# 225 products behind the last real one, with weights that lie apart, are one number, or are few

## The chip, the cores and the metric

The kernel runs on one core of a Trainium2 chip. The metric is the device time of one execution in microseconds (us); lower is better. The time of before is 3466.73 us, the median of two runs (3463.19 and 3470.27).

## What is computed

Two transformer-like networks, one behind the other, over one sequence of 512 tokens with 1024 features, in f32. The first has two layers of gated feed-forward, sparse attention beside a gating MLP, and feed-forward again. The second has two layers as well; its last piece, with which the kernel ends, is

```python
m_lat = sq_relu_mlp(modulate(rms_norm(x, g_mlp_pre[i]), sh2, sc2), w_mlp_in[i], w_mlp_out[i])
x = x + gt2 * rms_norm(m_lat, g_mlp_post[i])
```

where `sq_relu_mlp` is `square(relu(h @ w_in)) @ w_out` with 4096 hidden features. What is added by the change is no part of this: its results stay in two banks that nobody reads.

## The kernel before, in words

Activations lie feature-major: a tile `[128, 8, 512]` holds 8 blocks of 128 features by 512 tokens. Every matrix product of weights is made from three passes. ScalarE rounds a raw weight tile to `WH` (line 557, a type that TensorE streams at full rate), VectorE makes the rest `WL = raw - WH` (line 568), and the activations are split in the same way, into `nH` and `nL`. A product is then WH x nH + WH x nL + WL x nH, three matmuls that add up in one PSUM bank (lines 662 to 664, and likewise 1039 to 1041, 2483 to 2485, 2778 to 2780). In `pe.q.matmul(out, weights, moving)` the second argument is the stationary one, which is loaded into the array by a weight load (engine PEld in the profile), and the third is streamed past it, one column after the other. "512 columns" is the width of the moving argument. All weights of these products are `[128, 128]` pieces whose 128 numbers lie next to each other in each partition.

There are four buffers for `WH` and four for `WL` (`NW = 4`), each `[128, 2048]`, used in turn. `M.ones` is a `[128, 128]` f32 tile of ones; with it sums over partitions are made, and also products that only keep TensorE at work (`warm_up`, line 682, and line 1440).

Each engine has its program, a Python function that issues its instructions in the order in which they stand: `pe_program`, `act_program`, `dve_program`, `pool_program`, `sp_program`. Semaphores tie them together; `then_inc` counts one up, `wait_ge` waits for a value. PSUM has eight banks. Six go round in `now.order`: `take` hands out the next one and returns with it the event that empties it, on which the caller waits before it writes. Banks 6 and 7 hold the two `stat` tiles of the halves of the sequence.

TensorE's program ends in `rest_pe`, whose last call is `mlp2_turn_pe`, the last feed-forward. It ends in `turn_pe` (lines 2512 to 2533): eight blocks of 128 output features for the first half of the tokens, eight for the second, each of 24 matmuls of 256 columns (lines 2483 to 2485), and then the norm of the second half: `half_sum_pe` (line 877, sums by weights times a column of ones) and `half_spread_pe` (line 882, one product with the tile of ones, which spreads the inverse root over all partitions). VectorE adds each block into `ma` (line 2730 of `into_sums`, which empties the bank and counts up `v_h`), and at the very end multiplies by the spread norm (line 2696) and adds to `h` (line 2701), from where SyncE stores it.

The names of the change: `lat.nH` and `lat.nL` are the split activations, `[128, 8, 512]` each; `M.WH[0]` and `M.WL[0]` the first of the four weight buffers, which no later step of the kernel writes at that place; `mm` TensorE's semaphore.

Of the kernel before, what the change touches and what calls it, by code (L numbers as in the profile page):

```python
# [234 lines left out]
def drain(steps):  # L235
    for _ in steps:
        pass


def weave(main, side, pace):  # L240

    n, live = 0, [True, True]
    while live[0] or live[1]:
        for which, steps, c in ((0, main, 1), (1, side, pace(n) if live[0] else 1)):
            for _ in range(c):
                if live[which]:
                    try:
                        next(steps)
                    except StopIteration:
                        live[which] = False  # L250
        n += 1
# [158 lines left out]
def build(nc, A, out):  # L410
# [3 lines left out]
    with ctx:  # L414
        M = memory(nc, ctx)
        lat, con, key = M.lat, M.con, M.key
        sems = {}

        def sem(name):
            sems[name] = Sem(ctx.enter_context(nc.semaphore(name)))  # L420
            return sems[name]
# [15 lines left out]
        mm = sem("mm")  # L437
# [29 lines left out]
        def take(*group):  # L467

            b = now.order.pop(0)
            now.order.append(b)  # L470
            bank_of[group] = b
            before = now.holder.get(b)
            now.holder[b] = group
            if before is None:
                return banks[b], (mm.handle, 0)
            if COUNTING[0]:
                return banks[b], (mm.handle, 1)
            return banks[b], emptied_by[before].to(*before)
# [51 lines left out]
        offs, at = [], 0  # L530
# [1020 lines left out]
        def network_pe(pe, l, j):  # L1551
            g = f"ffn{l}{j}"
            if l == j == 0:
                start_pe(pe)
            else:
                enter_pe(pe, l, 2 * j)
            yield from ffn_pe(pe, g, lat, g, NF, True, "ffn_w_in", "ffn_w_out", M.hH, M.hL, l + j > 0, l * j == 0,
                              begun=l == j == 0)
# [672 lines left out]
        def mixer_pe(pe, l):  # L2231
            g = f"mix{l}"
            enter_pe(pe, l, 1)
            attention1_pe(pe, g, l)
            gmlp_pe(pe, g)
            for m in range(4):
                for which in range(2):
                    if m or which:
                        merge_pe(pe, g, which, m)
# [272 lines left out]
        def turn_pe(pe, post, g, group, clear):  # L2512

            A, B = lat.half

            def first_sum():
                pe.wait_ge(*clear[0])
                half_sum_pe(pe, post + "A", A)

            for o in range(8):  # L2520
                group(pe, 0, o)
            for o in range(8):
                group(pe, 1, o, first_sum if o == 0 else None)
                if o == 0:
                    half_spread_pe(pe, post + "A", A)
                if o == 5 and g is not None:
                    half_sum_pe(pe, g + "A", A)
                if o == 6 and g is not None:
                    half_spread_pe(pe, g + "A", A)
            pe.wait_ge(*clear[1])  # L2530
            if g is None:
                half_sum_pe(pe, post + "B", B)
                half_spread_pe(pe, post + "B", B)
# [204 lines left out]
        def mlp2_turn_pe(pe, g, after, lead):  # L2738
            yield from ffn_pe(pe, g, lat, g, NF2, False, "w_mlp_in_2", "w_mlp_out_2", M.hH2, M.hL2, lead > 0, True, lead)
            extra = narrow()  # L2740
            turn_pe(pe, g + "post", after, second_end_pe(g), [emptied(x) for x in extra])
# [138 lines left out]
        def context_pe(pe):  # L2880
            yield from pooled_pe(pe)
            yield from norm_pe(pe, "ctxmlp", con)
# [47 lines left out]
        def latents_pe(pe):  # L2930
            for s in range(LATENTS_STEPS):
                if s == 4:
                    b, free = take(FIN, "sum")
                    pe.wait_ge(*free)
                    pe.wait_ge(*v_ssum.to(FIN, 7))
                    pe.wait_ge(*v_ssum.to(POOL2, 7))
                    for j in range(4):
                        c = slice(j * 128, j * 128 + 128)
                        pe.q.matmul(b[:, j:j + 1], lat.scr[2][:, c], M.ones[:, 0:1], start=True, stop=True)
                        pe.q.matmul(b[:, 4 + j:5 + j], M.fin[2][:, c], M.ones[:, 0:1], start=True, stop=False)  # L2940
                        t = pe.q.matmul(b[:, 4 + j:5 + j], lat.scr[2][:, c], M.epsc[:, 0:1], start=False, stop=True)
                    t.then_inc(*mm.up(FIN, "sum"))
                if s == 5:
                    spread_pe(pe, POOL2, M.fin[3])
                    spread_pe(pe, FIN, lat.scr[3])
                    put_back(FIN, "rstd")
                if s == 8:
                    put_back(POOL2, "rstd")
                if s in POOLED_STEPS:
                    pool_out_pe(pe, POOL2, POOLED_STEPS.index(s), M.gH, M.gL, S)  # L2950
                if s == 19:
                    sum_pe(pe, POST2, M.fin[2])
                if s == 20:
                    spread_pe(pe, POST2, lat.scr[3])
                if s == 27:
                    put_back(POST2, "rstd")
                    sum_pe(pe, MLP2, M.fin[2])
                if s == 28:
                    spread_pe(pe, MLP2, lat.scr[3])
                if s == 32:  # L2960
                    put_back(MLP2, "rstd")
                yield
# [325 lines left out]
        def tail_pe(pe):  # L3288
            g, p = "ctxkey", key
            yield from norm_pe(pe, "ctxmlppost", p)  # L3290
            yield from norm_pe(pe, g, p)
            xs, ready = normed_x(p, g)
            slot_pair(pe, "w_qkv_2", C, xs, ready, [("kc0", "raw"), ("kc1", "raw")])
            yield
            slot_pair(pe, "w_qkv_2", C, xs, ready, [(g, "v", i) for i in range(2)])
            yield
            for name in ("kc0", "kc1"):
                head_pe(pe, p, name)
            yield
            values_pe(pe, g, p)  # L3300
            yield
            yield
            for name in ("kc0", "kc1"):
                head_spread_pe(pe, p, name)
            yield
# [43 lines left out]
        def latents_on_pe(pe):  # L3349
            yield from mlp2_turn_pe(pe, "latmlp0", "latatt", 0)  # L3350
# [303 lines left out]
        def rest_pe(pe, output):  # L3654
            turn_pe(pe, "wopost", "latmlp1", output, [a_ev.to("y2", hh) for hh in (6, 7)])
            after_turn_pe(pe, "w_mlp_in_2", "wopost", "latmlp1", FIRST_HIDDEN)
            drain(mlp2_turn_pe(pe, "latmlp1", None, 3))
# [35 lines left out]
        def beside_context(n):  # L3693
            return 1

        def pe_program(pe):
            pe.wait_ge(*v_one.to("ones"))
            for l in range(2):
                drain(network_pe(pe, l, 0))
                pe.wait_ge(*ld_id.to())  # L3700
                mixer_pe(pe, l)
                if l == 0:
                    drain(network_pe(pe, l, 1))
            weave(network_pe(pe, 1, 1), context_pe(pe), beside_network)
            weave(context_on_pe(pe), latents_pe(pe), beside_context)
            weave(latents_on_pe(pe), tail_pe(pe), beside_context)
            rest_pe(pe, attention2_pe(pe))

        def act_program(act):
            act.wait_ge(*v_one.to("eps"))  # L3710
            for l in range(2):
                drain(network_act(act, l, 0))
                act.wait_ge(*ld_vec.to())
                mixer_act(act, l)
                if l == 0:
                    drain(network_act(act, l, 1))
            weave(network_act(act, 1, 1), context_act(act), beside_network)
            weave(context_on_act(act), latents_act(act), beside_context)
            weave(latents_on_act(act), tail_act(act), beside_context)
            attention2_act(act)  # L3720
            rest_act(act)
# [105 lines left out]
        for program in (pe_program, act_program, dve_program, pool_program, sp_program):  # L3827
            program(Lane(Tally()))
# [3 lines left out]
        block = ctx.enter_context(nc.Block())  # L3832
# [114 lines left out]
```

## Time and profile before

| | us |
|---|---|
| median of the runs shown | 3466.73 |
| the profiled execution | 3466.52 |
| its span, first to last instruction | 3464.7 |
| TensorE busy | 3413.6 (99%) |
| weight loads busy | 2874.5 (83%) |
| VectorE busy | 2165.7 (63%) |
| ScalarE busy | 1318.4 (38%) |

The rows below come from that execution. A row of a timeline gives the start in us from the span's start, the duration, engine, line, operation and tiles. TensorE's matmuls are pipelined: a record lasts from its start to the end of its results, and the next one begins before that. So what a matmul costs in a stream is the distance between starts, not the duration of a record. A product of two plain f32 tiles (the ones) stands in the trace as two records. PEclk and the clock column are the clock that TensorE was granted, as a share of 2.4 GHz.

### The profile page before, as it was taken

The numbers are of one execution on the slowest core, as the hardware profiler recorded it, in microseconds if no ns is written. First come the engines' busy times: TensorE is split into PE (matmuls) and PEld (weight loads), VectorE is DVE, ScalarE is ACT, GpSimd is POOL, SyncE is SP. The second block draws the span as 40 slices with busy tenths as digits, with TensorE's granted clock in tenths as the row PEclk, the third lists the DMA queues.
The fourth block names the chain that finished last, engine by engine and source line by source line (L and its number), as shares of the span: only waits on it lengthen the run. The fifth ranks groups of instructions, "written<-read, shape, count | busy, mean of one in ns | idle before, by whom it ended". The sixth has DMA issues, their size and how long they took to land.

```text
span 3464.7 us, 46915 instructions
## 1 busy us (share of the span) xinstructions
PE 3413.6 (99%) x18494; PEld 2874.5 (83%) x18494; DVE 2165.7 (63%) x3570; ACT 1318.4 (38%) x1951; POOL 298.0 (9%) x376
## 2 busy tenths in 40 slices
PE   9999999999999999999999999999999999999998
PEld 7888967898888988896789888899988898588888
DVE  7555565656555655666577777888776556655444
ACT  4222463333222422245333523355533236643222
POOL 0000232001000100023100000012100001210000
PEclk9999999999999999999999999999999999999999
DMA  7444302434444344320243444344444311013221
GB/s 279 188 158 163 107 24 101 163 129 168 158 162 151 134 169 158 148 106 12 101 164 140 149 150 170 146 147 182 172 174 165 117 66 68 25 50 112 96 98 48
DMA packets 85561, 452.01 MB, mean 130 GB/s; under 512 B 10304, under 2 KB 12544, under 8 KB 48608
## 3 DMA queue, kind: packets, MB, share of 16 engines
q1 hardware_dynamic: 83168, 439.10, 34.2%
q0 software_dynamic: 2176, 9.92, 0.8%
q8 instruction: 148, 2.42, 0.3%
q14 instruction: 69, 0.57, 0.0%
HBM read 446.88 MB, written 2.10 MB: 130 GB/s over the span
## 4 chain that ended last, share of the span: by engine, by line
PE 84%; DVE 7%; ACT 3%; issue 2%; DMA 2%; POOL 0%; SPq 0%; DVEq 0%; ACTq 0%; POOLq 0%
PE ps L662 21%; PE ps L663 21%; PE ps L664 21%; DVE WL L568 2%; DMA araw<-in_ast 2%; PE ps L2778 1%; PE ps L2780 1%; PE ps L2779 1%; PE ps L3477 1%; PE ps L1039 1%; PE ps L1040 1%; PE ps L1041 1%; ACT P L1859 1%; PE ps L1776 1%; PE ps L1299 1%
## 5 line engine op out<-in xcount | busy, mean ns | idle before, releaser
L662 PE MATMUL ps<-nH,WH 128*128 128x512 f32 x2256 | 880.3, 390 | 0.4 <-ACT rot L3207 0.4
L664 PE MATMUL ps<-nH,WL 128*128 128x512 f32 x2256 | 877.8, 389 | 0.0
L663 PE MATMUL ps<-nL,WH 128*128 128x512 f32 x2256 | 877.8, 389 | 0.0
L568 DVE TENSOR_TENSOR WL<-raw,WH 128x2048 fp32r<-128x2048 f32 (+2 forms) x297 | 651.6, 2199 | 361.5 <-ACT WH L557 360.0
L557 ACT ACTIVATE WH<-raw 128x2048 fp32r<-128x2048 f32 (+2 forms) x299 | 543.2, 1822 | 561.1 <-PE ps L664 479.9
L662 PEld LDWEIGHTS ps<-nH,WH 128*128 128x128 f32 x2256 | 423.5, 188 | 90.6 <-issue 3.3
L664 PEld LDWEIGHTS ps<-nH,WL 128*128 128x128 f32 x2256 | 423.4, 188 | 88.3
L663 PEld LDWEIGHTS ps<-nL,WH 128*128 128x128 f32 x2256 | 423.5, 188 | 87.2 <-issue 0.2
L628 DVE SCALAR_TENSOR_TENSOR araw<-araw,cB 128x1024 f32<-128x1024 f32 x224 | 275.6, 1230 | 205.6 <-DMA araw<-in_ast 205.2
L662 PE MATMUL ps<-hH,WH 128*128 128x512 f32 x944 | 368.8, 391 | 2.5 <-DVE ma L2454 1.4
L664 PE MATMUL ps<-hH,WL 128*128 128x512 f32 x944 | 367.4, 389 | 0.0
L663 PE MATMUL ps<-hL,WH 128*128 128x512 f32 x944 | 367.2, 389 | 0.0
L1146 ACT ACTIVATE scr<-ps 128x512 f32<-128x512 f32 x152 | 89.5, 595 | 414.4 <-PE ps L664 387.2
L1012 POOL TENSOR_SCALAR scr<-scr,der,mods 128x256 f32<-128x256 f32 x112 | 86.2, 771 | 1805.8 <-DVE scr L925 1804.8
L1153 ACT ACTIVATE hH<-scr 128x512 fp32r<-128x512 f32 x152 | 95.8, 633 | 357.5 <-DVE scr L1199 355.5
L662 PEld LDWEIGHTS ps<-hH,WH 128*128 128x128 f32 x944 | 177.2, 188 | 40.3 <-DVE ma L2454 1.9
L664 PEld LDWEIGHTS ps<-hH,WL 128*128 128x128 f32 x944 | 177.2, 188 | 36.9
L663 PEld LDWEIGHTS ps<-hL,WH 128*128 128x128 f32 x944 | 177.2, 188 | 36.6
L1199 DVE TENSOR_TENSOR scr<-scr,ps 128x512 f32<-128x512 f32 x88 | 59.5, 687 | 108.4 <-PE ps L664 107.0
L1266 DVE SCALAR_TENSOR_TENSOR h<-ps,der,h 128x512 f32<-128x512 f32 x144 | 99.7, 746 | 27.2 <-PE ps L664 25.9
L1202 DVE TENSOR_TENSOR scr<-scr 128x512 f32<-128x512 f32 x64 | 43.1, 690 | 101.3 <-ACT scr L1146 100.9
L1208 DVE TENSOR_TENSOR hL<-scr,hH 128x512 fp32r<-128x512 f32 x152 | 100.8, 687 | 4.3
(452 smaller groups left out, 5940.0 us busy)
## 6 DMA issues: line engine op xcount, KB each, us to landing
raw<-in_wst SPq DMA_DIRECT2D x273, 1024.0 KB, 4.8
araw<-in_ast SPq DMA_DIRECT2D x225, 512.0 KB, 5.7
raw<-in_wst SPq DMA_DIRECT2D x18, 512.0 KB, 3.3
araw<-in_wst SPq DMA_DIRECT2D x9, 1024.0 KB, 4.8
row<-in_ast SPq DMA_DIRECT2D x15, 512.0 KB, 10.5
cw<-in_cw POOLq DMA_DIRECT2D x4, 1024.0 KB, 5.9
h<-in_xT SPq DMA_DIRECT2D x4, 512.0 KB, 5.6
raw<-in_wst SPq DMA_DIRECT2D x8, 256.0 KB, 2.6
```

Of the source, the lines that this page charges most:

```text
L557: act.q.activation(M.WH[k % NW][:, 0:n], M.raw[raw_use[k]][:, 0:n], ACT.Copy).then_inc(*a_whi.up(k))
L568: dve.q.tensor_tensor(M.WL[k % NW][:, 0:n], M.raw[raw_use[k]][:, 0:n], M.WH[k % NW][:, 0:n].bitcast(F32), ALU.subtract).then_inc(*v_wlo.up(k))
L628: dve.q.scalar_tensor_tensor(out=w[:, :], in0=w[:, :], scalar=1.0, in1=M.cB[q][:, :], op0=ALU.mult, op1=ALU.mult, accum_out=total).then_in ...
L662: pe.q.matmul(to, hi[:, i, cc], xh, start=i == 0, stop=False)
L663: pe.q.matmul(to, hi[:, i, cc], xl, start=False, stop=False)
L664: t = pe.q.matmul(to, lo[:, i, cc], xh, start=False, stop=i == nk - 1)
L1012: pool.q.tensor_scalar(p.scr[2 + i % 2][:, p.cols], p.scr[i % 2][:, p.cols], G[:, i:i + 1], shift[:, i:i + 1], ALU.mult, ALU.add).then_inc ...
L1146: act.q.activation(p.scr[n % 2][:, 0:N], bank(g, "a", ci, f)[:, 0:N], ACT.Silu if gated else ACT.Relu).then_inc(*empties(a_fn, g, "a", ci, f))
L1153: act.q.activation(hH[:, ci % 2, f, :], p.scr[(2 if gated else 0) + f % 2][:, 0:N], ACT.Copy if gated else ACT.Square).then_inc(*a_hhi.up( ...
L1199: dve.q.tensor_tensor(p.scr[2 + u][:, 0:N], p.scr[u][:, 0:N], bank(g, "b", ci, f)[:, 0:N], ALU.mult).then_inc(*empties(v_pr, g, "b", ci, f))
L1208: dve.q.tensor_tensor(hL[:, ci % 2, f, :], p.scr[2 + f % 2][:, 0:N], hH[:, ci % 2, f, :].bitcast(F32), ALU.subtract).then_inc(*v_hlo.up(g, ...
L1266: dve.q.scalar_tensor_tensor(out=M.h[:, o, :], in0=bank(g, "o", ci, o)[:, :], scalar=gate[:, o:o + 1], in1=M.h[:, o, :], op0=ALU.mult, op1 ...
```

## The change

A function `end_pe` is called as TensorE's last step, behind `rest_pe`. It takes two banks and issues, in this order:

- 20 times two products of ones by ones (`between`), into the second bank;
- 25 groups of nine products each into the first bank, each group followed by two products of ones. The nine are three blocks i = 0, 1, 2, and for each the three passes of a real product (WH x nH, WH x nL, WL x nH). The moving operand starts at number 512 i + 16 x `line` of the tile;
- one last product of ones, which counts up a semaphore for which nobody waits.

The groups differ in their weights and their columns:

| groups | columns | weights |
|---|---|---|
| 4 | 512 | 128, every second number of 256 |
| 4 | 512 | 128, every fourth number of 512 |
| 2 | 512 | 128 times one number |
| 2 | 512 | 64 next to each other |
| 1 | 512 | 32 next to each other |
| 8 | 256 | 128, every second number |
| 4 | 256 | 128, every fourth number |

```diff
+        def end_pe(pe):
+
+            nh, nl = (x[:, :, :].rearrange("p a b -> p (a b)") for x in (lat.nH, lat.nL))
+            two = [take("end", x) for x in range(2)]
+            for b, free in two:
+                pe.wait_ge(*free)
+            to, aside = two[0][0], two[1][0]
+
+            def between():
+                for _ in range(2):
+                    pe.q.matmul(aside[:, 0:128], M.ones[:, :], M.ones[:, :], start=True, stop=True)
+
+            def apart(w, i, step):
+                return w[:, 512 * i:512 * i + 128 * step].rearrange("p (a b) -> p a b", b=step)[:, :, 0]
+
+            def block(w, i, rows):
+                return w[:, 128 * i:128 * i + rows]
+
+            def one(w, i, _):
+                return w[:, 512 * i:512 * i + 1].broadcast_to([128, 128])
+
+            def nine(N, line, weights, how, rows=128):
+                for i in range(9):
+                    w, x = ((0, 0), (0, 1), (1, 0))[i % 3]
+                    at = 512 * (i // 3) + 16 * line
+                    pe.q.matmul(to[0:rows, 0:N], weights(M.WL[0] if w else M.WH[0], i // 3, how),
+                                (nl if x else nh)[:, at:at + N], start=i == 0, stop=i == 8)
+                between()
+
+            for _ in range(20):
+                between()
+            for line in range(4):
+                nine(512, line, apart, 2)
+            for line in range(4):
+                nine(512, line, apart, 4)
+            for line in (0, 1):
+                nine(512, line, one, 0)
+            for line in (0, 3):
+                nine(512, line, block, 64, 64)
+            nine(512, 0, block, 32, 32)
+            for line in range(8):
+                nine(256, line, apart, 2)
+            for line in (0, 1, 2, 3):
+                nine(256, line, apart, 4)
+            t = pe.q.matmul(aside[:, 0:128], M.ones[:, :], M.ones[:, :], start=True, stop=True)
+            t.then_inc(*mm.up("end", 1))
...
             rest_pe(pe, attention2_pe(pe))
+            end_pe(pe)
```

Line 3706 is the product of ones in `between`, line 3721 the product in `nine`, line 3740 the last one. On TensorE the seam between the old program and the new instructions looks so, with the semaphores that are waited for (`v_dg` is VectorE's count of the inverse roots; `WH_7` and `WL_11` are the first weight buffers):

```order
 L877 MATMUL ps<-ones,scr_26 128x1
 L882 MATMUL ps<-scr_27,ones 128x256 [waits v_dg]
+L3706 MATMUL ps<-ones 128x128 [waits v_h]
+L3706 MATMUL ps<-ones 128x128 x39
+L3721 MATMUL ps<-nH,WH_7 128x512
+L3721 MATMUL ps<-nL,WH_7 128x512
+L3721 MATMUL ps<-nH,WL_11 128x512
```

The first added instruction carries the only wait of the addition. Behind the last product of the last group, of 256 columns, TensorE's program now ends in this way, where `L414` is the end of the block for all engines:

```order
+L3721 MATMUL ps<-nH,WH_7 128x256
+L3721 MATMUL ps<-nL,WH_7 128x256
+L3721 MATMUL ps<-nH,WL_11 128x256
+L3706 MATMUL ps<-ones 128x128 x2
+L3740 MATMUL ps<-ones 128x128
 L414 UNCONDITIONAL_BRANCH
```

Nothing moved: before, the branch stood directly behind line 882. The orders of the other engines are the same but for line numbers, which are 48 higher behind the new function.

## Rows read from the trace of the kernel before

**Rows 1.** The page's head and its table of busy time by engine

```profile
span 3464.7 us, 46915 instructions
...
PE 3413.6 (99%) x18494; PEld 2874.5 (83%) x18494; DVE 2165.7 (63%) x3570; ACT 1318.4 (38%) x1951; POOL 298.0 (9%) x376
```

**Rows 2.** Groups by line and shape: out<-in, count | busy us, mean ns | idle before

```profile
L662 PE MATMUL ps<-nH,WH 128*128 128x512 f32 x2256 | 880.3, 390 | 0.4 <-ACT rot L3207 0.4
...
L1039 PE MATMUL ps<-nH,WH 128*128 128x256 f32 x320 | 92.1, 288 | 0.3
...
L1641 PE MATMUL ps<-R,cw 128*128 128x62 f32 x128 | 14.7, 273 | 0.0
...
L663 PEld LDWEIGHTS ps<-nL,WH 128*128 128x128 f32 x2256 | 423.5, 188 | 87.2 <-issue 0.2
...
L1039 PEld LDWEIGHTS ps<-nH,WH 128*128 128x128 f32 x320 | 61.4, 192 | 0.9 <-issue 0.8
...
L2101 PEld LDWEIGHTS ps<-wT,vn 128*64 128x64 f32 x128 | 6.9, 137 | 0.7 <-issue 0.7
```

**Rows 3.** Timeline of TensorE, first and last of 46 products of 512 columns

```profile
599.79 0.39 PE L662 MATMUL ps<-nH,WH 128*128 128x512 f32 x1
...
609.99 0.39 PE L662 MATMUL ps<-yaH,WH 128*128 128x512 f32 x1
```

**Rows 4.** Timeline of the tail, from the last products of 256 columns to the end

```profile
3450.81 0.28 PE L2484 MATMUL ps<-hL,WH 128*128 128x256 f32 x1
...
3452.01 0.28 PE L2485 MATMUL ps<-hH,WL 128*128 128x256 f32 x1
3452.33 0.42 DVE L2730 TENSOR_TENSOR ma<-ma,ps 128x256 f32<-128x256 f32 x1 [2.12 <-PE ps L2485]
...
3453.80 0.58 PE L877 MATMUL ps<-ones,scr 128*128 128x1 f32 x4 [1.51 <-DVE scr L908]
...
3455.45 1.22 PE L882 MATMUL ps<-scr,ones 128*128 128x256 f32 x2 [1.07 <-DVE scr L916]
3456.70 0.69 DVE L2696 TENSOR_TENSOR ma<-ma,ps 128x512 f32<-128x512 f32 x1 [1.31 <-PE ps L882]
...
3458.15 4.34 SPq L3820 DMA_DIRECT2D out<-h  x4
...
3461.40 0.69 DVE L2701 TENSOR_TENSOR h<-h,ma 128x512 f32<-128x512 f32 x1
```

**Rows 5.** Windows: stretch, its length, busy us (records) by engine, PEclk, DMA share, GB/s

```profile
3440.00:3446.00 6.00, 6.00 (x52) 6.00 (x51) 2.73 (x7) 1.86 (x4) 0.00 (x0) 1.00 0.21 68
3456.00:3465.00 9.00, 0.67 (x2) 0.00 (x0) 5.25 (x8) 0.00 (x0) 0.00 (x0) 0.50 0.34 117
...
600.00:609.90 9.90, 9.90 (x45) 8.20 (x44) 8.80 (x17) 0.59 (x2) 0.00 (x0) 1.00 0.00 0
...
18.80:21.30 2.50, 2.50 (x14) 2.50 (x13) 0.50 1.03 408
21.60:23.20 1.60, 1.60 (x15) 1.42 (x13) 1.00 1.06 266
```

**Rows 6.** Timeline of DVE: blocks 2 and 3 of the second half leave their banks

```profile
3437.93 0.42 DVE L2730 TENSOR_TENSOR ma<-ma,ps 128x256 f32<-128x256 f32 x1 [0.76 <-PE ps L2485]
...
3440.81 0.42 DVE L2730 TENSOR_TENSOR ma<-ma,ps 128x256 f32<-128x256 f32 x1 [0.41 <-PE ps L2485]
```

**Rows 7.** Timeline of TensorE near the start: products of ones

```profile
18.53 4.69 PE L682 MATMUL ps<-ones 128*128 128x128 f32 x28
...
26.23 3.29 PE L1440 MATMUL ps<-ones 128*128 128x128 f32 x28
```

**Rows 8.** Timeline of TensorE, first and last of nine products of the context

```profile
2349.17 0.28 PE L2779 MATMUL ps<-hLc,WH 128*128 128x256 f32 x1
...
2350.11 0.28 PE L2778 MATMUL ps<-hHc,WH 128*128 128x256 f32 x1
```

## Prediction

> **What bounds the kernel now.** I read the page's table of engines first. TensorE is busy 99% of a span of 3464.7 us with 18494 matmul records [rows 1], so anything that is put on TensorE and isn't beside a wait of TensorE lengthens the kernel. The change adds only TensorE work, and only behind the last instruction that TensorE has. So two things are to be read: what one product of each shape costs in a dense stream, and how much of the tail, in which TensorE is idle already, the addition can use.
>
> The mean durations by shape (390 ns for 512 columns, 288 ns for 256) [rows 2] are no prices, since records overlap. The price is the distance from start to start. In the timeline 45 products of 512 columns start between 599.79 and 609.99 us: 10.20 / 45 = 0.2267 us each [rows 3]. At 256 columns, 10 products start between 3450.81 and 3452.01 us: 0.1200 each [rows 4]. The difference, 106.7 ns for 256 columns, is 0.417 ns a column, one column per clock at the higher level of 2.4 GHz, at which these stretches are granted (1.00 in [rows 5]). What is left is a price per product that doesn't depend on its columns: 226.7 - 512 x 0.417 = 13.3 ns. On this number the forecast turns, because the new products change only their weights.
>
> The tail: TensorE's last real product starts at 3452.01 us. DVE, ACT and TensorE then pass the last norm to each other, TensorE's last two records (one product of `M.ones`) run from 3455.45 to 3456.67, and DVE and the output DMAs fill the rest up to 3464.7 [rows 4]. There the granted clock is 0.50, the lower level of 1.2 GHz [rows 5], after TensorE had been mostly idle from 3452.3 to 3455.45. So 3464.7 - 3456.5 = 8.2 us of the addition cost nothing, whatever it is.
>
> **The change part by part.** Nothing is removed or moved; the other engines' instructions stand as before. Four things are added.
>
> *The wait.* `end_pe` takes two banks and waits for `v_h`. The two that come next held blocks 2 and 3 of the second half, which DVE read (L2730) at 3437.93 and 3440.81 us [rows 6], over 14 us before TensorE gets there. The wait costs nothing, and nothing is queued behind it but the addition. No engine waits for the semaphore at its end. I let the addition start at 3456.5.
>
> *The 40 lead-in products of ones.* A product of two plain f32 tiles is two records in the trace: the 14 products of L1440 are 28 records, and they take 0.111 us each ((3.29 - 0.28) / 27) at the higher clock [rows 7]. At the lower level 14 records touch a stretch of 2.50 us where at the higher 15 touch 1.60 [rows 5], so about 0.2 each. How long the lower level lasts I take from the start of this kernel, where it is still 0.50 up to 21.30 and 1.00 from 21.60 the ones there having begun at 18.53 [rows 5, 7]: some 3 us. So of 80 records 14 at 0.213 and 66 at 0.1115: 3.0 + 7.4 = 10.4 us, up to 3466.9.
>
> *The separators.* 25 x 2 products are 100 records x 0.1115 = 11.15 us; the last product 0.22, and 0.28 until its record ends.
>
> *The 225 products.* If weights apart cost what contiguous ones do: 13 groups x 9 x 0.2267 = 26.52, and 12 x 9 x 0.1200 = 12.96. TensorE then ends at 3466.9 + 26.5 + 13.0 + 11.2 + 0.5 = 3518.1. The profiled execution took 3466.52 us over a span of 3464.7, so 1.8 lie around it, and its time is 0.2 below the median: 3519.9.
>
> No row of before shows weights that aren't contiguous, so their price is bounded. From below: the 13.3 ns go altogether, 225 x 13.3 = 3.0 us less (a gain). From above: a weight load is a record of 188 to 192 ns that today lies wholly beside the product before it [rows 2]; if none of it did, the 180 products with weights apart would cost 180 x 0.19 = 34 us more. Between them I ask what the 13.3 ns are. The timeline of the context's products has the same weight tiles, columns and engine but other moving tiles, and there 8 products take 2350.11 - 2349.17 = 0.94, 0.1175 each [rows 8]: the constant is 10.8 ns there. A price that depends on which tile streams past is not a fixed cost of an instruction; it looks like the reading of weights getting in the way of the reading of the moving tile. Then it should grow with the stretch of memory the weights lie in. I take that: x2 for every second number, x4 for every fourth, none for one number, a half and a quarter for 64 and 32. So +13.3 ns x (36 + 72) = 1.4 us, +40 ns x (36 + 36) = 2.9, -13.3 x 18 = -0.2, -6.7 x 18 - 10 x 9 = -0.2; together +3.9, and 3523.7 us. It is also near the middle of what is likely and far nearer to the free end than to 34.
>
> Weight loads of 64 columns take 137 ns against 192 for 128, 0.86 ns a column, and 128 products of only 62 columns still take 14.7 us, 0.115 each, much like the ones with their 0.111: there the loads of 128 columns set the pace [rows 2]. The Trainium skill, "TensorE: Matmul & The Clock Gate", section "LDWEIGHTS (loading the stationary operand)", has the same: the load's time is its columns over 1.2 GHz, and nothing else. By it alone weights apart are free, as in the first rival. Against this change stands "Advanced Engine Details and Errata", section "SBUF Cachelines": lines of 16 bytes, and a reader needs "at least two hits on a cacheline to absorb SRAM access latency". f32 at every second number is two hits a line, at every fourth one; no run here shows it yet.
>
> **The rivals.**
>
> 1. *Weights apart cost what contiguous ones do.* For it: loads have their own record beside the products and are off TensorE's path everywhere. Against it: 0.1175 against 0.1200 with equal shapes. 3519.9 us, still slower but within 2%.
>
> 2. *Loads at every fourth number take twice as long, and become the bound of the short products.* A load comes each 0.111 us at best; twice that, 0.223, hides behind 512 columns (0.2267) and not behind 256 (0.1200). Price: 36 x 0.103 = 3.7 us on top of rival 1: 3523.6. Only where the time sits tells it from my forecast. The rule on cachelines above would give this.
>
> 3. *The other side: loads of weights apart aren't hidden.* If a strided load holds up the product behind it by a load's whole pace, 180 x 0.1115 = 20.1 us more than rival 1: 3540.0, +2.1%, slower by over 2%. It decides from (3536.1 - 3519.9) / 180 = 0.09 us a product. For it speaks only that no strided load is in the trace; against it that loads begin with the product before them and have 0.2267 us of room at 512 columns, in 72 of the 180.
>
> 4. *The clock stays at its lower level.* Columns then cost 0.417 ns more: 117 x 512 and 108 x 256 columns make 25.0 + 11.5, and 100 records 0.1 more each, 10: about 3570 us, +3%. Against it: the same string of ones brings the clock back within some 3 us at the kernel's start [rows 5], and the products that follow have no wait among them.
>
> That the addition does nothing to the time can't be: it would have to fit into 8.2 us.
>
> **How the numbers follow.** Price by the stretch of memory (forecast, 3523.7): 0.38. Rival 1: 0.25. Rival 2: 0.20. Rival 3: 0.11. Rival 4: 0.03. What I haven't thought of: 0.03, of it 0.01 faster. The range goes from the free end (3519.9 less 3.0 for the constant and 1.4 if the clock never falls: 3515) to just under rival 3: 3539. It leaves out rivals 3 and 4 and the 34 us of the upper bound, some 0.17. By 2%, which is about what a measurement of this kernel can tell from no change, faster is below 3397.4 and slower above 3536.1: faster 0.01, same 0.85, slower 0.14.
>
> **What would show it.** Distances from start to start in the new groups. By my forecast at 512 columns: every second 0.240, every fourth 0.267, one number 0.213, 64 weights 0.220, 32 weights 0.217; at 256 columns 0.133 and 0.160. By rival 1: 0.227 and 0.120 throughout. By rival 2: 0.227 at 512 columns, and 0.223 for every fourth at 256, where every second stays at 0.120. By rival 3: 0.34 and 0.23. The lead-in should end about 11.5 us after TensorE's last record of before began, and the granted clock be 1.00 from the first group on. I am wrong in the main step if one number costs as much as 128 contiguous ones, or if every fourth costs the same as every second; wrong in the frame if the first added product waits, or if separators cost more than 0.1115 a record behind products of another kind.

## The result, and the profile after

The changed kernel takes 3523.72 us, the median of two runs (3522.63 and 3524.80), against 3466.73 before: a ratio of 1.0164, 95% interval 1.0118 to 1.0211. Run again beside the experiments, four times, it took 3523.69 (1.0165, 1.0148 to 1.0182). It is slower by 57 us. The second interval lies wholly under a ratio of 1.02; the first, of two runs, reaches just past it. The predicted time was 3523.7. That it fits so well is partly luck, as the terms below show: the step on which the sum turned was wrong.

The profiled execution of after is the one of 3522.63 us. The head of its page answers to [rows 1]; TensorE has 407 records more, 225 products and twice 91 products of ones.

```profile
span 3520.8 us, 47730 instructions
...
PE 3481.1 (99%) x18901; PEld 2937.4 (83%) x18901; DVE 2166.2 (62%) x3570; ACT 1319.1 (37%) x1951; POOL 298.9 (8%) x376
```

Windows of the new tail answer to [rows 5]; the columns are those of there.

```profile
3453.10:3456.40 3.30, 3.30 (x14) 3.12 (x15) 2.07 (x4) 0.00 (x0) 0.00 (x0) 0.50 0.00 0
3456.50:3464.00 7.50, 7.50 (x70) 7.50 (x69) 3.08 (x5) 0.00 (x0) 0.00 (x0) 1.00 0.43 142
3464.00:3520.00 56.00, 56.00 (x327) 50.98 (x326) 0.00 (x0) 0.00 (x0) 0.00 (x0) 1.00 0.00 1
```

The clock is low for some 3 us, comes back early among the ones and stays. VectorE and the output are done under the lead-in. From 3464 on TensorE alone works, with no gap.

The chain of work that ended last is the best view for the groups, because it gives each group's time from end to end: start, us, what. The 13 groups of 512 columns, then the 12 of 256:

```profile
3453.01 1.22 PE ps L882 x2
3454.23 10.03 PE ps L3706 x80
3464.25 2.11 PE ps L3721 x9
3466.37 0.44 PE ps L3706 x4
...
3474.43 2.23 PE ps L3721 x9
...
3485.19 2.07 PE ps L3721 x9
...
3490.25 2.06 PE ps L3721 x9
...
3497.85 1.08 PE ps L3721 x9
...
3510.08 2.11 PE ps L3721 x9
...
3520.30 0.22 PE ps L3740 x2
```

They are the first groups of their kinds: every second number (3464.25), every fourth (3474.43), one number (3485.19), 64 weights (3490.25), and at 256 columns every second (3497.85) and every fourth (3510.08). Nine products of 256 columns take 1.08, as contiguous ones would (9 x 0.120), with every second number, and 2.11 with every fourth: 0.234 a product, twice the price, and as much as 512 columns cost. One number at 512 columns takes 2.07, not 1.92.

The groups by weight load say why. The first row is of the stretch of 512 columns at every second number, the second of every fourth at 512, the third of every second at 256, the fourth of every fourth at 256.

```profile
L3721 PEld LDWEIGHTS ps<-nL,WH 128*128 128x128 f32 x12 | 2.3, 196 | 0.3
...
L3721 PEld LDWEIGHTS ps<-nL,WH 128*128 128x128 f32 x12 | 3.8, 317 | 0.0
...
L3721 PEld LDWEIGHTS ps<-nL,WH 128*128 128x128 f32 x24 | 4.7, 196 | 0.0
...
L3721 PEld LDWEIGHTS ps<-nL,WH 128*128 128x128 f32 x12 | 4.0, 331 | 0.0
```

Contiguous weights were 188 to 192 [rows 2]. Every second number adds some 5 ns, every fourth 120 to 140.

### The profile page after: what moved, and what is told of

It is laid out like the page before. It is cut to its first block, busy times and chain, and to the rows that moved or that the text cites. A ratio compares the mean times of both kernels' runs of the same rounds, so it can differ in the third digit from the quotient of the medians.

```text
span 3520.8 us, 47730 instructions
## 1 busy us (share of the span) xinstructions
PE 3481.1 (99%) x18901; PEld 2937.4 (83%) x18901; DVE 2166.2 (62%) x3570; ACT 1319.1 (37%) x1951; POOL 298.9 (8%) x376
## 4 chain that ended last, share of the span: by engine, by line
PE 86%; DVE 6%; ACT 3%; issue 2%; DMA 1%; POOL 0%; SPq 0%; DVEq 0%; ACTq 0%; POOLq 0%
PE ps L662 21%; PE ps L664 21%; PE ps L663 21%; PE ps L2778 1%; PE ps L2780 1%; PE ps L2779 1%; DVE WL L568 1%; PE ps L3721 1%; PE ps L3477 1%; DMA araw<-in_ast 1%; PE ps L1039 1%; PE ps L1040 1%; PE ps L1041 1%; PE ps L1776 1%; ACT P L1859 1%
```

## The experiments

Theory L, formed from these rows: a load of weights at every fourth number has half the pace, and a product costs the larger of its load and its columns; the 13.3 ns of [rows 3, 4] have nothing to do with weights. Theory S is the one that I predicted with: the 13.3 ns grow with the stretch of memory that the weights lie in. All kernels change `end_pe` alone; the kernel's real work is untouched, and the results of the added products are read by nobody. The kernels from "Long runs" on were timed once each, and only distances inside their traces are read.

**The changed kernel again**

No edit.

> The changed kernel unaltered, beside the two that follow, so that they have one chip and one time to be compared with. Every theory: 3523.7 us within 2; the start-to-start distances as in its first trace, by group about 0.233 (512 columns, every second number), 0.238 (every fourth), 0.231 (one number, 64, 32 weights), 0.120 (256 columns, every second), 0.234 (256 columns, every fourth).

Measured: 3523.69 us (3521.48 to 3526.46), each group within 0.03 us of the first trace.

**Weights next to each other**

```diff
-            for line in range(4):
-                nine(512, line, apart, 2)
-            for line in range(4):
-                nine(512, line, apart, 4)
+            for line in range(8):
+                nine(512, line % 4, block, 128)
...
-                nine(256, line, apart, 2)
+                nine(256, line, block, 128)
...
-                nine(256, line, apart, 4)
+                nine(256, line, block, 128)
```

> All weights that lie apart are replaced by 128 that lie next to each other; the groups, columns, moving tiles and separators stay. Theory L (a load at every fourth number has half the pace, every second number is free, and the 13.3 ns have nothing to do with the weights): the eight groups of 512 columns take 2.49 to 2.55 us each with their separators, the twelve of 256 columns 1.53 each, so only the eight groups at every fourth number give something back, 4 x 0.15 + 4 x 1.02 = 4.7 us, and the kernel takes 4 to 6 us less than the changed one. Theory S (my prediction: the 13.3 ns grow with the stretch of memory the weights lie in): 3.9 us less than the changed one, of which 1.4 from the groups at every second number, whose short groups fall from 1.65 to 1.53. Rival N (strided weights cost nothing and the long groups are slow for another reason): the same time within 1 us.

Measured: 3519.86 us (3517.05 to 3520.15), 3.8 less than the changed kernel on the same chip. The chain, with a group of 512 columns in place of every second number, one in place of every fourth, and the same at 256 columns:

```profile
3463.78 2.08 PE ps L3721 x9
...
3473.91 2.07 PE ps L3721 x9
...
3496.67 1.08 PE ps L3721 x9
...
3508.73 1.07 PE ps L3721 x9
```

What falls is what L says: the groups at every fourth number, by 1.05 us at 256 columns and 0.16 at 512 on average, together 4.8. Every second number gives back only 0.01 to 0.02 a group: at 256 columns the eight groups took 1.08 or 1.09 and take 1.04 to 1.08 now. By the medians alone L and S, 4.7 and 3.9, can't be told apart; by the rows S falls, for it wanted 1.20 (9 x 0.133) where 1.08 stood. N falls too.

**No lead-in**

```diff
-            for _ in range(20):
-                between()
```

> The 40 products of ones ahead of the groups are left out; the groups follow the last real product at once. If the clock comes back with any dense work: some 10.0 us of lead-in go, and the first 2 to 5 us of products run at the lower level at twice their time, which gives back 1.2 to 2.5: 7.5 to 9 us less than the changed kernel. If it takes the string of ones to bring the clock back (the groups stay at the lower level): 117 x 0.213 + 108 x 0.107 + 100 x 0.1 = 46 us more instead of 10 less, 36 us more than the changed kernel.

Measured: 3516.12 us (3510.19 to 3519.75), 7.6 less. The windows of the first group and of the next four have the clock at 0.50 and at 1.00:

```profile
3455.00:3457.70 2.70, 2.70 (x8) 2.11 (x7) 2.63 (x5) 0.00 (x0) 0.00 (x0) 0.50 0.26 89
3458.50:3468.90 10.40, 10.40 (x55) 9.36 (x53) 1.49 (x3) 0.00 (x0) 0.00 (x0) 1.00 0.21 71
```

In the chain the first group alone is slow:

```profile
3454.60 3.64 PE ps L3721 x9
```

The second takes 2.10 again. The lead-in's term was right, and rival 4 falls: products bring the clock back as ones do. A side result counts later. The timeline has the group's inner products, of which the second and the eighth are

```profile
3454.82 0.63 PE L3721 MATMUL ps<-nL,WH 128*128 128x512 f32 x1
...
3457.38 0.63 PE L3721 MATMUL ps<-nL,WH 128*128 128x512 f32 x1
```

At the lower level they start 2.56 / 6 = 0.427 us apart, which is 512 columns at 1.2 GHz and nothing on top. The 13.3 ns are gone there.

**Long runs**

```diff
+            run(45, 512, block, 128)
+            run(45, 512, block, 32, 32)
+            run(45, 512, one, 0)
+            run(45, 512, apart, 2)
+            run(45, 512, block, 128, one_moving=True)
+            run(45, 512, block, 128, bank=(to, aside))
+            run(45, 512, block, 128, tile=M.hH2[:, :, :, :].rearrange("p a b c -> p (a b c)"))
+            run(45, 384, block, 128)
+            run(45, 256, block, 128)
+            run(45, 256, block, 32, 32)
+            run(45, 256, one, 0)
```

These stand in place of the groups.

> Instead of the 25 groups eleven runs of 45 products each, with two products of ones behind each. 512 columns: 128 contiguous weights; 32 weights; one number; every second number; contiguous with one moving tile throughout; contiguous with two banks in turn; contiguous with the hidden activations as moving tile. Then 384 and 256 columns contiguous; 256 with 32 weights; 256 with one number. Theory L, 13.3 ns is not the weights': contiguous, 32, one number and every second number all settle at 0.2267 at 512 columns, 0.120 at 256, and 384 columns take 0.1733. Theory S: one number 0.2133 to 0.216, 32 weights 0.217, every second number 0.240. If the 13.3 ns come from adding up in one bank, the run with two banks settles near 0.216; if from reading two moving tiles in turn, the run with one tile does; if from where the moving tile lies, the run with the hidden activations differs from the first. If the 0.231 to 0.233 of the groups of nine is a matter of being short, each run begins so and settles within some ten products.

Measured, from the chain: 512 columns with 128 contiguous weights, with one number, with every second number; then 256 columns with contiguous weights and with one number:

```profile
3465.54 10.25 PE ps L3734 x45
...
3487.11 10.43 PE ps L3734 x45
...
3497.98 10.50 PE ps L3734 x45
...
3549.22 5.40 PE ps L3734 x45
...
3560.63 5.12 PE ps L3734 x45
```

Contiguous weights begin between 0.22 and 0.24 and settle at 0.2267 after some ten products; so a group of nine never gets to the price that [rows 3] show. One number, and 32 weights in the same way (10.43), don't settle and stay at 0.232, dearer than 128; every second number stays at 0.233. At 256 columns it is the other way round: one number takes 5.12 / 45 = 0.1138, 32 weights too, against 0.1200 for 128. Neither L, by which the weights don't count, nor S, by which fewer are always cheaper, has these 5 to 6 ns, and no later run explains them. 384 columns take 7.81 / 45 = 0.1736, which is still 384 x 0.417 + 13.3. The bank, one moving tile or two, and the tile itself make no difference (10.23 or 10.24).

**Spacing of the weights**

```diff
+            for step in (1, 2, 3, 4, 5, 6, 8, 15):
+                nine(128, 0, step)
+            for at in (1, 2, 3):
+                nine(128, at, 3)
+            for step in (1, 2, 3, 4, 5, 6, 8, 15):
+                nine(256, 0, step)
+            for at in (1, 2, 3):
+                nine(256, at, 3)
+            for n in (64, 32):
+                nine(256, 0, 4, False, n)
+            for N in (128, 256):
+                for step in (1, 2, 4, 6, 8, 16):
+                    nine(N, step > 1, step, True)
```

In place of the groups; `True` is bf16, with ones as moving tile.

> Groups of nine as in the change, one for each spacing of the weights. First 128 columns, f32 at every 1st, 2nd, 3rd, 4th, 5th, 6th, 8th, 15th number, then every 3rd from numbers 1, 2, 3; the same at 256 columns; 64 and 32 weights at every 4th number at 256 columns; then bf16 weights (one bf16 is half an f32) at every 1st, 2nd, 4th, 6th, 8th, 16th at 128 and 256 columns. Theory P (a pair rule: two weights within 16 bytes load at full pace, one weight per 16 bytes at half): at 128 columns 0.111 for 1st and 2nd, something between for 3rd, 0.233 for 4th and everything beyond, with no further growth; bf16 slow from the 8th on, not at the 4th. Theory G (pace grows with the stretch): 3rd about 0.17, 4th 0.23, 8th 0.46, 15th 0.9. Theory C (a count of numbers, not bytes): bf16 is slow from the 4th on like f32. 64 and 32 weights at every 4th number at 256 columns: loads need half and a quarter of the time and hide, about 0.120, by P and C.

Measured: at 128 columns the first four groups, every 1st, 2nd, 3rd, 4th number; then at 256 columns the 4th and 15th; then bf16 at 128 columns, 6th and 8th:

```profile
3467.06 0.96 PE ps L3718 x9
...
3468.51 1.01 PE ps L3718 x9
...
3470.02 1.51 PE ps L3718 x9
...
3472.03 2.10 PE ps L3718 x9
...
3501.21 2.11 PE ps L3718 x9
...
3511.39 2.10 PE ps L3718 x9
...
3526.09 0.50 PE ps L3718 x9
...
3527.09 0.55 PE ps L3718 x9
```

The distances inside the first four are 0.111, 0.118, 0.173 and 0.234. 128 weights at every 2nd, 3rd, 4th number touch 64, 96, 128 stretches of 16 bytes, and 118 / 64 = 1.84, 173 / 96 = 1.80, 234 / 128 = 1.83 ns. So a load of this type costs the larger of its columns (0.111) and some 1.82 ns for each 16 bytes that it touches. Beyond every 4th nothing grows with the spacing (2.06 to 2.18 from the 5th to the 15th): G falls. bf16 is slow only from the 8th on, which is 16 bytes again: C falls. But it is slow at another price: 0.55 / 9 = 0.061 us for 128 stretches is 0.48 ns each, where 1.82 would make 0.233. Why a bf16 load is so much quicker is open; the 1.82 ns are shown for weights of the kernel's type alone. 64 and 32 weights at every 4th number hide, 1.06 and 1.07. P is right, for this type in a sharper form. The Trainium skill has the 16 bytes and the two hits ("Advanced Engine Details and Errata", section "SBUF Cachelines"), and this trace agrees, with 1.82 ns as the price for this type. The statement of the Trainium skill that a load's time is its columns ("TensorE: Matmul & The Clock Gate", section "LDWEIGHTS (loading the stationary operand)") holds only for weights next to each other.

**Columns**

```diff
+            for step in (1, 4):
+                for N in (128, 192, 256, 320, 384, 448, 480, 512):
+                    for line in (0, 1):
+                        nine(N, line, apart, step)
```

> Contiguous weights, then every fourth number, at 128, 192, 256, 320, 384, 448, 480 and 512 columns, two groups of nine each. Theory L (a load at every fourth number is slow by itself, and a product costs the larger of its columns and its load): every fourth 0.233 at all widths up to 480, 0.238 at 512; contiguous 0.111 at 128 and 192 (load), 0.117 to 0.120 at 256, then 0.147, 0.173, 0.200, 0.213, 0.230. Rival K (strided loads are slow only because they meet the stream of the moving tile): every fourth grows with the columns, below 0.17 at 128 columns and near 0.233 only at 256 and beyond.

Measured: every fourth number at 128 and 384 columns, first group each:

```profile
3497.20 2.05 PE ps L3721 x9
...
3517.67 2.16 PE ps L3721 x9
```

Behind the first product, which starts late, the distance is on average 0.233 to 0.236 up to 384 columns and 0.234 to 0.239 from 448 on. The load is slow by itself; K falls. Contiguous weights fit at 320 and 384 columns (0.147, 0.174), but at 448 one of two groups took 0.206 and at 480 both took 0.218, more than columns plus 13.3.

**Steps of 16 columns?**

```diff
+            for spread in (0, 1):
+                for N in (248, 252, 256, 260, 264, 272, 288, 496):
+                    run(27, N, 0, spread)
+            for spread in (0, 1):
+                for start in (1, 4, 8, 16, 32):
+                    run(27, 256, start, spread)
```

`spread` 0 is one number as weights, 1 is 128 contiguous ones.

> What the 13.3 ns behind the columns are. Runs of 27 products at 248, 252, 256, 260, 264, 272, 288 and 496 columns, first with one number as weights and then with 128 contiguous ones; then at 256 columns with the moving tile beginning 1, 4, 8, 16 and 32 numbers further on, again with both kinds of weights. Theory Q (a product takes whole steps of 16 columns, 6.7 ns, and one or two steps more than its columns): one number gives 0.1133 for 248, 252 and 256 columns and 0.120 for 260 to 272, in steps. Theory F (a fixed price on top of the columns): 0.417 ns for each column, 248 and 256 columns 3.3 ns apart. If the reading of weights gets in the way of the moving tile only where both begin alike, the runs with contiguous weights vary with the start and those with one number don't.

Measured with one number, at 248, 260, 288 and 496 columns:

```profile
3468.66 3.06 PE ps L3714 x27
...
3479.25 3.22 PE ps L3714 x27
...
3490.42 3.56 PE ps L3714 x27
...
3494.43 6.11 PE ps L3714 x27
```

That is 0.1133, 0.1193, 0.1319 and 0.2263 a product: not steps, and not a fixed price, for what is left over the columns is 10 ns at 248 and 20 at 496. But divided by the stretches of 16 bytes of the *moving* tile, 62, 65, 72 and 124, it is 1.83 ns each time. Of the other four widths three lie between 1.82 and 1.84, and 256 columns at 1.79. With 256 columns (64 stretches) runs lie between 0.1141 and 0.1226 by start and weights; at each of the six starts the contiguous weights are dearer than one number, by 1 to 5 ns, while at 496 columns they are cheaper (0.2233). So the weights keep a small say, which no run explains. Q and F are both wrong, and 1.83 is the price that a stretch of weights of this type has, too.

**The moving tile**

```diff
+            run(27, every(1, 512))
+            run(27, one_number(512))
+            run(27, each(4))
+            run(27, again(4))
+            run(27, every(1, 256))
+            run(27, one_number(256))
+            for step in (2, 3, 4, 8):
+                run(27, every(step, 256))
+            for step in (2, 4, 8):
+                run(27, every(step, 256, 1), kind=BF16)
+            for step in (1, 2, 4):
+                run(9, every(step, 256), kind=F32)
```

> The weights are 128 contiguous ones throughout; what changes is how the moving tile lies in memory, in runs of 27 products (the last three of 9). 512 columns: contiguous; one number for all columns; 128 numbers, each four times in a row; 128 numbers gone through four times. 256 columns: contiguous; one number; every 2nd, 3rd, 4th, 8th number. bf16 at 256 columns: every 2nd, 4th, 8th. Plain f32 (two records a product) at 256 columns: every 1st, 2nd, 4th. Theory R (TensorE reads a stretch of 16 bytes, four f32, in about 1.82 ns whatever it takes from it; a product costs the larger of its columns at 0.417 ns with 2.5 on top, the stretches of its moving tile and those of its weights): 512 contiguous 0.227 to 0.233; one number 0.216; each four times 0.216; gone through four times 0.227 to 0.233; 256 contiguous 0.117 to 0.120; one number 0.111; every 2nd 0.233, 3rd 0.350, 4th and 8th 0.466; bf16 2nd 0.117, 4th 0.233, 8th 0.466; plain f32 0.215, 0.233, 0.466. Rival F (the 13.3 ns are a fixed price of a product of this type): 0.227 and 0.120 for one number as for contiguous, and strides of the moving tile of any price. Rival H (only the weights' reader has a pace by stretches): the moving tile's spacing changes nothing.

Measured, the four runs of 512 columns; 256 columns contiguous, from one number, and at every 2nd and 4th number; bf16 at every 2nd, 4th and 8th:

```profile
3463.33 6.14 PE ps L3722 x27
...
3469.91 5.85 PE ps L3722 x27
...
3476.21 5.83 PE ps L3722 x27
...
3482.48 6.14 PE ps L3722 x27
...
3489.07 3.24 PE ps L3722 x27
...
3492.75 3.02 PE ps L3722 x27
...
3496.21 6.12 PE ps L3722 x27
...
3509.34 6.29 PE ps L3722 x27
...
3522.41 3.06 PE ps L3722 x27
...
3525.91 6.16 PE ps L3722 x27
...
3532.52 12.21 PE ps L3722 x27
```

512 columns from 128 numbers, each four times in a row, take 0.2159, and from one number 0.2167: columns plus 2.6 to 3.4 ns. The same 128 numbers gone through four times, 128 stretches again, take 0.227, as contiguous ones do (6.14 both). 256 columns from one number take 0.112, contiguous 0.120. So the 13.3 ns are, but for those 3 ns, the reading of the moving tile and no fixed price: F falls. bf16 at every 2nd, 4th, 8th number takes 0.113, 0.228, 0.452, which is 64, 128 and 256 stretches at 1.77 to 1.78 ns each; plain f32 0.216, 0.227, 0.451 a record. H falls. R fails at one place: the products' own type at every 3rd, 4th and 8th number takes 0.227, 0.233 and 0.218 where R wanted 0.350 and 0.466. Why that type reads spaced columns faster than the others is open, and so for this type the price by stretches is shown only for moving tiles that are contiguous, repeated, or at every 2nd number.

## Why the prediction was right, and where it was wrong

The terms, forecast against the profiled execution of after. The times are from one chain start to that of the next kind.

| term | forecast us | measured us |
|---|---|---|
| start of TensorE's last product of before | 3455.45 | 3453.01 |
| from there to the first group | 11.45 | 11.24 |
| 512 columns, every second, 4 groups | 10.4 | 10.18 |
| 512 columns, every fourth, 4 groups | 11.4 | 10.76 |
| one number, 64, 32 weights, 5 groups | 12.0 | 12.66 |
| 256 columns, every second, 8 groups | 13.2 | 12.23 |
| 256 columns, every fourth, 4 groups | 7.5 | 10.22 |

**What bounds the kernel** held: nothing on another engine came into play, and the time is TensorE's. **The wait** held: the added instructions follow the last real one with no gap. **The lead-in** held within 0.3 us, and its removal gave 7.6 where 7.5 to 9 was expected. **The separators** held: 0.44 for four records, 0.111 each.

**The step that failed** is this: "it looks like the reading of weights getting in the way of the reading of the moving tile. Then it should grow with the stretch of memory the weights lie in." The forecast put 13.3 ns a product on the weights and scaled them. By the last two experiments the 13.3 ns at 512 columns are the moving tile's own reading, 128 stretches of 16 bytes at 1.77 ns instead of 512 columns at 0.417. With one number as weights they don't go: its groups took 2.07 and 2.09 us and contiguous ones 2.07 to 2.11, the sign that I had named for being wrong in the main step. Two widths, 512 and 256, gave me a slope and an offset, and 384 columns, at 0.1736, lie on the same line; it took 248 and 496 columns, 10 and 20 ns over their columns, and moving tiles that lie otherwise to show that the offset is no fixed price. The observation under the step, that the context's tile has another price [rows 8], was sound, and pointed to the moving side.

The weights do cost by the stretch of memory, but in their own reading, beside the products: 1.82 ns for each 16 bytes, 118 ns at every second number and 234 at every fourth, which shows only where it is more than the product costs. So every second number is hidden under 0.120 but for some 2 ns, and every fourth is not. That is rival 2, forecast at 0.223 a product and measured at 0.234, with its price where it put it: the short groups at every fourth number cost 1.05 us more each than contiguous ones, 4.2 in all, where my theory had 0.36 each. I gave it 0.20.

The sum came out because the errors cancel. The four short groups at every fourth number are 2.7 under; the eight at every second are 0.9 over, the first two kinds 0.9 over, one number and few weights 0.7 under. These sum to 1.6 too little, and this execution's real work ended 2.4 us earlier than the one I started from, with 0.2 from the lead-in: 3523.7 + 1.6 - 2.6 = 3522.7, against 3522.63. The 0.2 us by which the profiled execution lies below the median stand in the forecast's words, but not in its 3519.9. A size not in any forecast is that groups of nine are too short to settle, 2.52 us where nine times 0.2267 and the separators make 2.49.

Rival 1 gave 3519.9 us, which is what the kernel with contiguous weights takes (3519.86); for the changed kernel it is 3.8 us short. Rival 3, loads that aren't hidden, is wrong: at 512 columns every fourth number cost 0.16 us a group, not 1.0. Rival 4 is wrong by the run without lead-in. The range held, and the chances by 2% were placed rightly: the price that would have crossed it, 0.09 us on each of 180 products, came on 36 of them only.

## What to carry to other kernels

Price a matmul of this kernel's type in a dense stream by the largest of three: its columns, the 16-byte stretches of its moving operand, and those of its weights (here 1.77 to 1.84 ns each). Behind the first product of a group that comes out within 10 ns in these runs, with two exceptions: a moving operand of this type at every 3rd number or further apart costs less, and bf16 weights have a lower price. Weights at every second f32 are free to within 2 ns in the short groups and cost 6 ns in a long run of 512 columns; at every fourth they cost a product of 256 columns twice its time. bf16 weights became dearer only at every 8th number, by 6 ns at 128 columns. A line through a few widths doesn't make what is left over a fixed price: let the operand lie otherwise in memory and see whether it goes. And check groups one by one in the chain, since a total can be right for wrong reasons.

## What was not expected

A dense stream without a wait can lose the clock. In the run on spacing, with 128 columns, the granted clock fell to 0.50 during the group at every fourth number, stayed there for 23.7 us, and came back behind the first group of 256 columns, whose weights are contiguous:

```profile
3466.90:3473.30 6.40, 6.40 (x48) 6.40 (x46) 0.00 (x0) 0.00 (x0) 0.00 (x0) 1.00 0.00 0
3473.50:3497.20 23.70, 23.70 (x110) 23.70 (x110) 0.00 (x0) 0.00 (x0) 0.00 (x0) 0.50 0.00 1
```

TensorE is "busy" in every one of these, because records overlap, though a product of 128 columns started there only each 0.21 to 0.24 us. In the run on columns two groups of 128 and two of 192 columns at every fourth number, 10 us in all, kept 1.00; why the clock fell in the one run and not in the other is open. The numbers of the 128-column groups beyond every fourth are from the lower level and aren't used above.

The pace at which the moving tile is read does not follow that clock: in the run with bf16 at every 8th number the clock fell on the way (1.00 up to 3537.5, 0.50 from 3537.6 on), and its products started 0.452 us apart on both sides of it. At the lower level a column takes 0.427 us / 512 = 0.833 ns, four of them 3.3, more than the 1.77 of a stretch, so the reading would be hidden; that fits the 13.3 ns that vanished in the run without lead-in. Loads were not followed across the change in this way: 128 columns with weights at every 3rd number took 0.173 at the higher level and 0.213 at the lower.
